# Forty-five products of constants taken out of a fused two-block transformer kernel

## The chip, the cores and the metric

The kernel runs on one NeuronCore of a Trainium2 chip. The metric is device time in microseconds (us) of one launch, the median of several runs. Matrix products run on TensorE (PE in the profile, its weight loads PEld), element-wise work on VectorE (DVE) and ScalarE (ACT); SyncE (SP) issues the transfers of weights.

## What is computed

All in float32, 256 tokens of width 1024. The first block runs four recurrent branches on the same input, merges them by gates, adds the result to the input and normalises it (layer norm 1); a mixture of 32 experts (4 per token) and a gated projection of a side input follow, and layer norm 2. The second block puts 16 learned tokens in front (272 in all) and runs two layers, each half a gated feed-forward network, a mixer (sparse attention and retention in the first, sliding-window attention and pooling in the second, "odd" one), and half a network again. What matters here, from the reference:

```
def _layernorm(x, g, b, dtype):
    xf = x.astype(F32)
    xc = xf - jnp.mean(xf, -1, keepdims=True)
    var = jnp.mean(xc * xc, -1, keepdims=True)
    return (xc * lax.rsqrt(var + LN_EPS) * g + b).astype(dtype)
...
    logits = (xf @ router_w + router_b).astype(F32)
    top_val, top_idx = lax.top_k(logits, TOP_K)
```

## The kernel before

Activations lie transposed in the on-chip memory: 128 partitions of features, 8 tiles deep (`DT`), tokens along the free axis. The program is a list of stages (`STAGES`); each ends in `end_stage` (L771), where PE, ACT and DVE drain and wait for each other. Inside a stage every engine has a list of its own, in the order written, and the lists meet only at semaphores (`Signal`: `post` and `take`).

All large weights are one stream of 2 MB chunks, which SP puts into a ring in the order of use (L3305 for the first stages, L3335 and L3339 for the rest). SP waits before each chunk until PE has left its place; PE waits for a chunk at its first tile (`Weights.take`). So PE pulls the transfers after it, or is held by them. Nearly every product against weights is recorded at L307, in the helper `matmul`. Each product of float32 operands appears in the trace as two MATMUL passes, each with a weight load.

**A layer norm** (`LayerNorm`, L657). PE sums the features by products with a matrix of ones (L673), DVE centres (L700), ACT squares (L687), PE sums the squares, again with ones (`square_sums`, L677, recorded at L681). Then comes a chain off PE: DVE adds the epsilon (L705), ACT takes the root (L689), DVE inverts (L707), DVE scales the eight tiles (L710), and ACT adds beta to each tile (L694).

`idle_products` (L766, recorded at L769) multiplies a constant matrix of ones by a constant identity, 128x128 by 128x128, into a bank of the accumulators in which nothing is kept at that moment. It waits for nothing, posts nothing, and nothing reads what it writes. It is called in three places:

- `merge_and_router` (stage 5, L1828): 13 products after the square sums of layer norm 1. Next on PE is `gate(0)`. It waits for each tile k of the normalised x, multiplies it for both halves of the tokens with the router's weights (stationary x, 32 columns: four passes, L1837), and multiplies the gate's weights with it (256 columns: two passes, L307). Seven more gates follow (`gate(1)` to `gate(7)`) without router products. The experts stage comes next.
- `second_norm` (stage 7, L2307): 28 products after the square sums of layer norm 2. Next on PE is the end of the stage, then the first feed-forward network (`swiglu`), whose products wait for x times a gain (DVE, L2365).
- `odd_mixer` (L3199): 4 products, after one projection step that PE does beside (`beside.next`, L307), and in front of the wait for the normalised queries and keys and of the attention (`attn.tensor`, its first products at L2514).

Of the kernel before, what the change touches and what calls it, by code (L numbers as in the profile page):

```python
# [19 lines left out]
P = 128  # L20
# [271 lines left out]
def new_signal(K, name):  # L292

    sem, count = K.spare.pop() if K.spare else (K.new_semaphore(name), 0)
    K.counts.append(Signal(sem, count))
    return K.counts[-1]
# [8 lines left out]
def matmul(K, out, lhsT, rhs, start, stop, signal=None):  # L305

    ins = K.nc.tensor.matmul(out, lhsT, rhs, start=start, stop=stop)  # L307
    if signal is not None:
        ins.then_inc(*signal.post())
    elif K.weights.pending is not None:  # L310
        ins.then_inc(K.weights.used[K.weights.pending], 1)
        K.weights.pending = None
    return ins
# [176 lines left out]
def flat(ap):  # L490
    return ap.rearrange("p a t -> p (a t)")
# [222 lines left out]
class HeadNorm:  # L714
# [45 lines left out]
    def spread_to(self, dve, j):  # L760

        dve.wait_ge(*self.ready.take())
        return self.K.bank[self.banks[j % len(self.banks)]][:, 0:T2]


def idle_products(K, bank, n):  # L766

    for _ in range(n):
        K.nc.tensor.matmul(K.bank[bank][:, 0:P], K.con["ones"][:, :], K.con["eye"][:, :], start=True, stop=True)  # L769


def end_stage(K):

    K.stages += 1
    n = K.stages
    recycle(K)

    @K.block.tensor
    def _(pe):
        pe.drain().then_inc(K.stage_done, 1)  # L780
        pe.wait_ge(K.stage_done, 3 * n)

    @K.block.scalar
    def _(act):
        act.drain().then_inc(K.stage_done, 1)
        act.wait_ge(K.stage_done, 3 * n)

    @K.block.vector
    def _(dve):
        dve.drain().then_inc(K.stage_done, 1)  # L790
        dve.wait_ge(K.stage_done, 3 * n)

    @K.block.gpsimd
    def _(pool):
        pool.wait_ge(K.stage_done, 3 * n)
# [21 lines left out]
def load(K, pairs):  # L817
    @K.block.gpsimd
    def _(pool):
        for dst, src in pairs:  # L820
            pool.dma_start(dst, src).then_inc(K.small_loaded, 16)
    K.small_loads += len(pairs)
# [948 lines left out]
def merge_and_router(K):  # L1771

    nc, block, bank, col = K.nc, K.block, K.bank, K.col
    T = T1
    with ExitStack() as st:
# [28 lines left out]
        eye = K.con["eye"][:, :]  # L1804
# [5 lines left out]
        def _(pe):  # L1810
# [13 lines left out]
            for j in range(DT):  # L1824
                for k in range(2):
                    matmul(K, p_at(j), K.weights.take(pe), p_in[:, k, :], k == 0, k == 1, p_ready if j == DT - 1 and k == 1 else None)
            ln.square_sums(pe)
            idle_products(K, 6, 13)  # L1828

            def gate(j):  # L1830
                if j >= 2:
# [439 lines left out]
def second_norm(K):  # L2271

    nc, block, bank, col = K.nc, K.block, K.bank, K.col
    with ExitStack() as st:
        ln = LayerNorm(K, st, "l2", K.acc[:, :, :], 4, 5, 1e-5)
        link = new_signal(K, "l2_dve_chain")
        load(K, [(K.x[:, :, 0:META], K.dram["meta"])])
        loads = 16 * K.small_loads
        turned, added = new_signal(K, "l2_turned"), new_signal(K, "l2_added")

        def out(j):
            return K.x[:, j, META:T2]

        @block.tensor
        def _(pe):
            def turn(q):
                for j in (2 * q, 2 * q + 1):
                    for b in range(2):
                        ins = nc.tensor.transpose(bank[q][:, j % 2 * T1 + b * P:j % 2 * T1 + (b + 1) * P], K.moe[:, b, j * P:(j + 1) * P],
                                                  K.con["eye"][:, :])  # L2290
                ins.then_inc(*turned.post())

            def mean(q):
                pe.wait_ge(*added.take())
                ln.mean(pe, 2 * q)
                ln.mean(pe, 2 * q + 1)

            turn(0)
            turn(1)
            mean(0)  # L2300
            turn(2)
            mean(1)
            turn(3)
            mean(2)
            mean(3)
            ln.square_sums(pe)
            idle_products(K, 6, 28)  # L2307

        @block.scalar
        def _(act):  # L2310
            ln.squares(act)
            ln.shift(act, out, "ln2_b")

        @block.vector
        def _(dve):
            for q in range(4):
                dve.wait_ge(*turned.take())
                part = flat(K.acc[:, 2 * q:2 * q + 2, :])
                dve.tensor_tensor(out=part, in0=part, in1=bank[q][:, :], op=ALU.add).then_inc(*added.post())
            dve.wait_ge(*added.posted())  # L2320
            ln.centre(dve)
            ln.scale(dve, out, "ln2_g")
            dve.wait_ge(K.small_loaded, loads)
    end_stage(K)
# [805 lines left out]
def odd_mixer(K):  # L3130
    nc, block, bank, col = K.nc, K.block, K.bank, K.col
    T = T2
    with ExitStack() as st:
# [33 lines left out]
        @block.tensor  # L3167
        def _(pe):
            def mix(j):
                pe.wait_ge(*pool_ready.take())  # L3170
                if j >= 2:
                    pe.wait_ge(*mix_free.take())
                nc.tensor.matmul(bank[j % 2][:, 0:T], dmix[:, j, :], pooled[:, j, :], start=True, stop=True).then_inc(*mix_ready.post())

            for j in range(10):
                columns.tensor(pe, 7 - j % 2, first=K.rms.hn_ready if j in (0, 2) else None, x=y if j < 2 else None)
                if j == 4:
                    pe.wait_ge(K.small_loaded, loads)
                if j > 4:
                    heads.gather(pe, j - 5)  # L3180
                if j > 5:
                    mix(j - 6)
            for k in range(DT):
                w = K.weights.take(pe)
                for b, (t0, tn) in enumerate(Q3):
                    matmul(K, bank[v_banks[b]][0:tn, 0:P], hn[:, k, t0:t0 + tn], w, k == 0, k == DT - 1, v_ready if k == DT - 1 else None)
                if k == 1:
                    heads.gather(pe, 5)
                if k == 4:
                    pe.wait_ge(*mix_free.take(2))  # L3190
                    heads.spread(pe, 0)
                if k > 4:
                    heads.spread(pe, k - 4)
            heads.spread(pe, 4)
            heads.spread(pe, 5)
            columns.until(pe, 10)
            beside.next(pe)
            pe.wait_ge(*v_free.take(3))
            idle_products(K, 5, 4)  # L3199
            pe.wait_ge(*qk_ready.take())  # L3200
            attn.tensor(pe)

# [213 lines left out]
```

## Time and profile before

| | |
|---|---|
| median of 3 runs | 2989.92 us |
| lowest, highest | 2985.75, 2990.21 us |
| the profiled execution | 2988.2 us, of which the span is 2986.4 us and 1.8 us lie around it |
| granted TensorE clock over the span | 0.989 |
| busy share of the span: PE, PEld, DVE, ACT, POOL | 97%, 64%, 27%, 12%, 1% |
| instructions | 35599 |

The span is what the trace covers; starts in the rows are us from its beginning. The granted clock is 1.00 for 2.4 GHz and 0.50 for 1.2 GHz. A busy share of PE says that products were under way, not that they ran at the full clock. A stage's loss counts where PE, or what PE waits for, is the chain that sets the end.

### The profile page before, as it was taken

How to read it: one execution, taken by the hardware profiler on the slowest of the kernel's cores; microseconds unless marked ns; L12 is line 12 of the kernel's file. 1: busy time of each engine (PE TensorE's matmuls, PEld its weight loads, DVE VectorE, ACT ScalarE, POOL GpSimd, SP SyncE). 2: the span in 40 equal slices, each digit the busy share in tenths (PEclk: the TensorE clock that was granted, in tenths of full speed). 3: DMA queues.
4: the chain of work that ended last, by engine and by line, in shares of the span. 5: the costliest groups of instructions: out<-in, count | busy, mean ns of one | idle time of the engine just before them, and what ended most of it. 6: DMA issues, size and time to landing. Idle time of an engine off the chain costs nothing.

```text
span 2986.4 us, 35599 instructions
## 1 busy us (share of the span) xinstructions
PE 2899.7 (97%) x14805; PEld 1911.9 (64%) x14806; DVE 817.3 (27%) x1864; ACT 361.6 (12%) x738; POOL 28.6 (1%) x56
## 2 busy tenths in 40 slices
PE   8999999989999999999999999999999999998999
PEld 7867778833333333333338888776788888876887
DVE  2546441222222222222223111642211111034110
ACT  1122320200000000000002000122000000012000
POOL 0000000000000000000000000000000000000000
PEclk9999999999999999999999999999999999999999
DMA  5122234569999999999994334331333333331430
GB/s 202 59 86 103 92 141 153 197 238 422 428 429 428 428 429 428 429 428 428 428 428 163 141 141 153 113 113 65 113 141 141 141 141 141 141 136 70 157 141 15
DMA packets 49532, 654.92 MB, mean 219 GB/s; under 512 B 5841, under 2 KB 8033, under 8 KB 10225
## 3 DMA queue, kind: packets, MB, share of 16 engines
q1 hardware_dynamic: 45248, 642.90, 53.6%
q0 software_dynamic: 3136, 9.38, 1.0%
q8 instruction: 87, 1.43, 0.2%
q10 hardware_dynamic: 1040, 1.05, 0.1%
q14 instruction: 21, 0.16, 0.0%
HBM read 652.26 MB, written 1.05 MB: 219 GB/s over the span
## 4 chain that ended last, share of the span: by engine, by line
PE 85%; DMA 8%; DVE 5%; ACT 1%; issue 1%; PEldq 0%; SPq 0%; DVEq 0%; PEld 0%; ACTq 0%
PE bank L307 72%; DMA weight_ring<-weight_stream 7%; PE bank L1104 2%; PE bank L2115 1%; PE bank L2084 1%; DVE expert_hidden L2216 1%; DVE expert_hidden L2217 1%; PE bank L2106 1%; PE bank L2348 1%; PE bank L1357 0%; ACT expert_y_slots L2162 0%; DVE mlstm_qk L1482 0%; PE bank L728 0%; DMA first_weight_ring<-weight_stream 0%; PE bank L3013 0%
## 5 line engine op out<-in xcount | busy, mean ns | idle before, releaser
L307 PE MATMUL bank<-ffn_x_gained,weight_ring 128*128 128x272 f32 (+1 forms) x2816 | 638.3, 389 | 3.1 <-DVE ffn_x_gained L2365 3.1
L307 PEld LDWEIGHTS bank<-ffn_x_gained,weight_ring 128*128 128x128 f32 x2816 | 534.7, 190 | 105.2 <-DVE ffn_x_gained L2365 4.6
L307 PE MATMUL bank<-weight_ring,expert_x_slots_t 128*64 128x512 f32 x2048 | 459.6, 600 | 3.5 <-DMA weight_ring<-weight_stream 3.5
L307 PEld LDWEIGHTS bank<-weight_ring,expert_x_slots_t 128*64 128x64 f32 x2048 | 141.3, 138 | 318.9 <-issue 306.0
L307 PE MATMUL bank<-x,first_weight_ring 128*128 128x256 f32 x1376 | 315.6, 385 | 20.4 <-DMA first_weight_ring<-weight_stream 12.7
L307 PE MATMUL bank<-ffn_h,weight_ring 128*128 128x272 f32 (+1 forms) x1408 | 322.0, 389 | 2.1 <-DVE ffn_up L2461 2.1
L307 PEld LDWEIGHTS bank<-ffn_h,weight_ring 128*128 128x128 f32 x1408 | 267.2, 190 | 54.0 <-DVE ffn_up L2461 3.8
L307 PEld LDWEIGHTS bank<-x,first_weight_ring 128*128 128x128 f32 x1376 | 261.6, 193 | 62.3 <-issue 23.4
L307 PE MATMUL bank<-weight_ring,expert_hidden_slots_t 128*64 128x512 f32 x1024 | 225.2, 592 | 0.0
L307 PEld LDWEIGHTS bank<-weight_ring,expert_hidden_slots_t 128*64 128x64 f32 x1024 | 73.4, 137 | 146.4 <-issue 123.7
L307 PE MATMUL bank<-even_hn,weight_ring 128*128 128x272 f32 x624 | 155.1, 404 | 0.0
L2226 DVE TENSOR_TENSOR moe_rows<-moe_rows,bank 128x512 f32<-128x512 f32 x128 | 79.4, 682 | 269.0 <-PE bank L2115 269.0
L307 PEld LDWEIGHTS bank<-even_hn,weight_ring 128*128 128x128 f32 x624 | 118.8, 195 | 28.9 <-issue 5.0
L2461 DVE TENSOR_TENSOR ffn_up<-bank,x_rms 128x272 f32<-128x272 f32 (+1 forms) x88 | 38.5, 438 | 273.7 <-PE bank L307 273.7
L2447 ACT ACTIVATE ffn_silu<-ffn_silu 128x272 f32<-128x272 f32 (+1 forms) x88 | 37.5, 426 | 567.1 <-DVE ffn_silu L2459 567.1
L2459 DVE TENSOR_TENSOR ffn_silu<-bank,x_rms 128x272 f32<-128x272 f32 (+1 forms) x88 | 38.5, 438 | 224.5 <-PE bank L307 224.4
L2470 DVE SCALAR_TENSOR_TENSOR x<-bank,x 128x272 f32<-128x272 f32 (+1 forms) x32 | 14.0, 437 | 313.5 <-PE bank L307 313.5
L307 PE MATMUL bank<-expert_b_gu,expert_select 32*64 32x512 f32 x256 | 70.5, 627 | 8.4 <-issue 8.4
L2216 DVE TENSOR_SCALAR expert_hidden<-bank 128x512 f32<-128x512 f32 x32 | 22.1, 692 | 195.8 <-PE bank L307 195.8
L2084 PE MATMUL bank<-x_rows,expert_pick 128*64 128x512 f32 x256 | 69.0, 618 | 0.0
L2115 PE MATMUL bank<-expert_y_slots,expert_spread 64*128 64x512 f32 x256 | 63.6, 615 | 3.5
L2158 ACT ACTIVATE expert_sigmoid<-expert_gate_part 128x512 f32<-128x512 f32 x32 | 20.2, 630 | 343.5 <-DVE expert_gate_part L2212 343.5
(600 smaller groups left out, 2181.9 us busy)
## 6 DMA issues: line engine op xcount, KB each, us to landing
weight_ring<-weight_stream SPq DMA_DIRECT2D x276, 2048.0 KB, 14.5
first_weight_ring<-weight_stream SPq DMA_DIRECT2D x30, 2048.0 KB, 7.8
x<-x_t SPq DMA_DIRECT2D x1, 1024.0 KB, 5.8
out_t<-x ACTq DMA_DIRECT2D x1, 1024.0 KB, 5.4
c_ret_ret_q<-const_ret_q POOLq DMA_DIRECT2D x1, 544.0 KB, 5.0
c_ret_ret_k<-const_ret_k POOLq DMA_DIRECT2D x1, 544.0 KB, 5.6
c_odd_pool_inv<-const_pool_inv POOLq DMA_DIRECT2D x1, 544.0 KB, 3.8
c_hgrn_hgrn_levels<-const_hgrn_levels POOLq DMA_DIRECT2D x1, 512.0 KB, 3.6
```

The source lines that it names most:

```text
L307: ins = K.nc.tensor.matmul(out, lhsT, rhs, start=start, stop=stop)
L1104: ins = nc.tensor.matmul(out(h), lhsT(h), rhs(h), start=start, stop=stop)
L2084: ins = nc.tensor.matmul(bank[3][rows[g], :], pick[:, b, :], K.x_rows[:, b, g * HW:(g + 1) * HW], start=b == 0, stop=b == 1)
L2106: ins = nc.tensor.transpose(bank[5][:, j * P:(j + 1) * P], h[:, 0, j * P:(j + 1) * P], eye)
L2115: ins = nc.tensor.matmul(bank[4 + 2 * b + g][:, :], spread_t[rows[g], b * P:(b + 1) * P], ys[rows[g], :], start=True, stop=True)
L2216: then(dve.tensor_scalar(h[:, 0, :], bank[1][:, :], 7.0, -7.0, ALU.min, ALU.max))
L2217: dve.scalar_tensor_tensor(out=h[:, 0, :], in0=h[:, 0, :], scalar=1.0, in1=gate[:, 0, :], op0=ALU.add, op1=ALU.mult)\
L2226: ins = dve.tensor_tensor(out=part, in0=part, in1=bank[4 + n][:, :], op=ALU.add)
L2348: self.K.nc.tensor.matmul(self.K.bank[6][:, 0:T2], self.K.con["ones"][:, :], self.sq[:, j % 2, :], start=j == 0, stop=j == DT - 1)\
L2447: act.activation(s[:, j % 2, :], s[:, j % 2, :], ACT.Silu).then_inc(*s_ready.post())
L2459: dve.tensor_tensor(out=s[:, j % 2, :], in0=bank[2 * (j % 2)][:, 0:T], in1=rms.rstd[:, t0:T2], op=ALU.mult).then_inc(*g_scaled.post())
L2461: dve.tensor_tensor(out=up[:, j % 2, :], in0=bank[2 * (j % 2) + 1][:, 0:T], in1=rms.rstd[:, t0:T2], op=ALU.mult).then_inc(*h_free.post())
```

## The change

The function and its three calls are deleted. 13, 28 and 4 products go, together 90 MATMUL passes with as many weight loads. Nothing is put in their place; no semaphore, buffer or order of other work is touched.

```
-def idle_products(K, bank, n):
-
-    for _ in range(n):
-        K.nc.tensor.matmul(K.bank[bank][:, 0:P], K.con["ones"][:, :], K.con["eye"][:, :], start=True, stop=True)
...
             ln.square_sums(pe)
-            idle_products(K, 6, 13)
...
             ln.square_sums(pe)
-            idle_products(K, 6, 28)
...
             pe.wait_ge(*v_free.take(3))
-            idle_products(K, 5, 4)
             pe.wait_ge(*qk_ready.take())
```

## Rows read from the trace of the kernel before

**Rows 1.** The page: span, PE, chain that ended last by engine

```profile
span 2986.4 us, 35599 instructions
PE 2899.7 (97%) x14805; PEld 1911.9 (64%) x14806; DVE 817.3 (27%) x1864; ACT 361.6 (12%) x738; POOL 28.6 (1%) x56
...
PE 85%; DMA 8%; DVE 5%; ACT 1%; issue 1%; PEldq 0%; SPq 0%; DVEq 0%; PEld 0%; ACTq 0%
```

**Rows 2.** The source line L769: the deleted products' passes, in ns

```profile
L769 PE MATMUL bank<-c_eye,c_ones x90: 273/275/275, 572.9 to 2690.0; 128*128 128x128 f32 x90
```

**Rows 3.** The chain around layer norm 1: start us, us, what

```profile
569.61 3.47 PE bank L681 x16
...
576.32 0.52 ACT x L694
...
576.88 0.63 PE bank L1837 x4
...
583.66 7.42 PE bank L307 x34
```

**Rows 4.** Windows there: length, busy by engine, then PEclk, DMA share, GB/s

```profile
575.95:576.87 0.92, 0.01 (x1) 0.00 (x0) 0.92 (x3) 0.56 (x2) 0.00 (x0) 1.00 0.01 0
576.88:583.66 6.78, 6.78 (x47) 6.42 (x48) 2.17 (x6) 4.02 (x8) 0.00 (x0) 1.00 0.67 242
```

**Rows 5.** Windows of the experts stage

```profile
660.00:663.00 3.00, 3.00 (x10) 0.77 (x8) 0.00 (x0) 0.00 (x0) 0.00 (x0) 0.50 0.00 0
...
700.00:1577.00 877.00, 861.21 (x3924) 283.33 (x3921) 230.07 (x545) 75.69 (x126) 0.95 (x1) 1.00 1.01 428
```

**Rows 6.** The chain around layer norm 2

```profile
1571.77 3.73 PE bank L681 x16
...
1582.72 4.39 PE bank L307 x18
```

**Rows 7.** The chain from there, its longest piece

```profile
1593.99 106.10 PE bank L307 x463
```

**Rows 8.** Windows of the second norm's deleted products

```profile
1575.10:1581.75 6.65, 6.64 (x58) 6.41 (x56) 5.43 (x10) 3.43 (x9) 0.00 (x0) 1.00 0.29 121
```

**Rows 9.** The chain in front of the odd attention

```profile
2686.81 0.51 DVE odd_cq_ck L3239
2687.36 1.99 PE bank L307 x8
2689.36 0.89 PE bank L769 x8
2690.25 0.47 PE bank L2514 x4
```

**Rows 10.** Windows where PE sits idle and the clock then falls

```profile
653.40:658.10 4.70, 0.00 (x0) 0.00 (x0) 3.02 (x10) 0.00 (x0) 0.00 (x0) 1.00 0.94 397
658.20:665.00 6.80, 6.02 (x14) 1.56 (x16) 0.48 (x2) 0.00 (x0) 0.00 (x0) 0.50 0.22 51
```

**Rows 11.** Windows on both sides of other falls and rises

```profile
310.00:310.80 0.80, 0.80 (x6) 0.80 (x6) 0.00 (x0) 0.00 (x0) 0.00 (x0) 0.50 0.00 0
310.85:316.70 5.85, 5.85 (x15) 4.68 (x16) 0.00 (x0) 0.18 (x1) 0.00 (x0) 0.50 0.00 0
...
1558.00:1562.60 4.60, 1.79 (x8) 0.49 (x6) 2.56 (x7) 0.33 (x1) 0.00 (x0) 1.00 1.01 431
1562.70:1566.00 3.30, 2.99 (x11) 2.48 (x12) 1.38 (x2) 0.00 (x0) 0.95 (x1) 0.50 0.99 422
...
1857.60:1863.00 5.40, 5.40 (x15) 4.13 (x13) 0.97 (x4) 0.00 (x0) 0.00 (x0) 0.50 0.01 3
...
2699.35:2706.10 6.75, 5.51 (x21) 3.76 (x18) 5.04 (x19) 2.89 (x12) 0.00 (x0) 0.50 0.00 0
...
2729.50:2733.40 3.90, 3.90 (x9) 3.18 (x10) 0.07 (x1) 0.00 (x0) 0.00 (x0) 0.50 0.00 0
```

**Rows 12.** Groups by line and form, 306.5 to 309.9 us: an 8-column product

```profile
L1541 PE MATMUL bank<-mlstm_w_gates,x 128*128 128x8 f32 x28 | 3.3, 257 | 1.3 <-PEq L780 1.3
```

## The prediction

> **What bounds the kernel now.** I read the page first. PE is busy for 97% of the span and holds 85% of the chain that ended last; DMA holds 8%, all other engines 7% [rows 1]. So the question at each of the three places is whether PE is on the chain there, and at what clock it runs. The line of the deleted products shows 90 passes of 275 ns [rows 2]. They overlap: eight of them take 0.89 us of the chain [rows 9], 0.111 us each, so the three groups last about 2.9, 6.2 and 0.9 us.
>
> Then I read the chain at each place. At the first norm PE ends the square sums at 573.08 (569.61 + 3.47) and reappears on the chain at 576.88 with the router's products, released by ACT's first tile at 576.84 [rows 3]. The 3.80 us between belong to DVE and ACT; the 13 products lie beside that chain, and PE is idle for only 0.92 us after them, with the clock at 1.00 [rows 4]. At the second norm PE ends the sums at 1575.50 and reappears at 1582.72, 7.2 us later; DVE's and ACT's steps and at last the stage's end are the chain between [rows 6], and the 28 products run beside them at full clock and end before 1581.75 [rows 8]. In front of the odd attention it is otherwise: DVE ends the last query tile at 2687.32, PE the projection step at 2689.35, and the four products stand on the chain for 0.89 us until the attention's first product at 2690.25 [rows 9].
>
> Last, the granted clock. After each of the first two places PE alone is the chain for long: `gate(0)` fills 6.78 us, all busy and at 1.00 [rows 4], the next gates follow at once [rows 3], and behind the second norm one piece of PE's chain runs for 106.1 us [rows 7]. A low clock there is paid in full.
>
> **The change, part by part.** What goes from the chain directly is 0.89 us at the odd attention [rows 9]. What is late next there is nothing on another engine: the queries were ready 2 us earlier, PE goes straight from the projection step to the attention. At the norms the direct gain is nothing: DVE and ACT cover the products, and they do the same work without them. What the products do is keep PE streaming, so I price the clock.
>
> *Does it fall?* Twice the trace shows PE going idle and the clock then falling: PE's last product in one case ended near 1559.8 and the clock was 0.50 from about 1562.7, 2.9 us later [rows 11]; in the other it ended near 653.4 and the clock was still 1.00 until 658.1, 4.7 us later, and 0.50 from then on [rows 10]. The second norm's 7.2 us exceed both: it falls there before PE resumes. The first norm's 3.80 us lie between the two: it falls within the wait or up to 0.9 us after `gate(0)` begins. I take 0.5 us.
>
> *What does low clock cost?* At 0.50, 15 passes of the gates' kind (128x256) touch 5.85 us [rows 11], about 0.39 us each; at 1.00, 34 took 7.42 us, 0.218 us each [rows 3]. Half of a low stretch is loss.
>
> *How long, where dense products follow?* Where PE resumes with full products, and no narrow ones ran before, the clock rose 3.30 and 3.90 us into them; where they followed a run of narrow products, of 8 columns in the case at 310 us, only 5.40 and 5.85 us into them [rows 11]. Half of that is 1.6 to 2.9 us. For the second norm I take 2.2 us, inside the two ends, nearer to the dense ones that it resembles.
>
> *How long in `gate(0)`?* It isn't dense: of its six passes per tile four have 32 columns. The nearest rows stand on two sides. The dense resumptions above give half of 3.3 us, 1.6 us. On the other side, 28 passes of 8 columns, each with a weight load of 128, kept PE busy for 3.3 us before 309.9 us [rows 12], and the clock fell while they ran, to 0.50 at 310.0, and stayed there through the remaining ones and 5.85 us of dense work [rows 11]. Being busy alone didn't help there. Were the clock held low for all of `gate(0)`, its 6.78 us [rows 4] would double: +6.8 us, less 0.5 us for the late fall, and then the dense gates would run low for a while, 1.6 to 2.9 us more, of which I take 2.3. That is 8.6 us, with 7.4 and 9.7 as ends. A pass of 32 columns with a 128-column weight load is nearer to the 8-column ones than to the dense ones in how little it streams between loads, so I take this side.
>
> The Trainium skill, "TensorE: Matmul & The Clock Gate", section "What's actually happening", has the gate follow how busy PE has recently been, and says beside it that instructions aren't counted; read so, the unbroken stream of `gate(0)` would release the clock as dense work does, and the first norm would cost 1.6 instead of 8.6 us. The 8-column stretch differs from that reading, since the clock fell under it. The sum below stands without this paragraph.
>
> *Is the first norm's loss absorbed?* From 700 to 1577 us the transfers run at 428 GB/s without a break [rows 5]: the experts are bound by DMA. But at 660 to 663 us nothing is transferred while PE works [rows 5]; the ring is full and SP waits for PE. The continuous stretch begins when PE frees places, so a late PE makes it begin late, and end late. No absorption: the loss before it is carried whole. From 1577 us on the ring is full again, and PE sets the pace.
>
> *Clock in the odd attention.* It already falls twice there, with 6.75 us low the first time, 5.51 of them busy [rows 11]. In front of the wait the four products make way for the attention's first scores and the next dense step, so PE streams about as much. I take no change; a fall that comes earlier and lasts once more would cost half of 5.51, 2.8 us, so this place gives -0.9 to +1.9 us.
>
> **Sum:** 8.6 + 2.2 - 0.9 = +9.9 us. Against the profiled execution's own 2988.2 us that is 2998.1 us; the median of the runs lies 1.7 us higher, which gives 2999.8. I forecast 2999 us. A measurement of this kernel can tell about 0.2%, 6 us, from no change.
>
> **Rivals.** *The clock comes back within `gate(0)`.* Its products leave no gap, and the wide ones are half of its time. Against it stand the 8-column stretch and the long rise after it. It gives 1.6 + 2.2 - 0.9 = +2.9 us, 2991 us (ends +2.3 and +4.9 with each norm at 1.6 to 2.9). This is also the time by the skill's rule named above. It decides if in the changed trace the clock is 1.00 before the last router product.
>
> *Not slower: the clock doesn't fall at the first norm, and what falls at the second is small.* The wait of 3.80 us is shorter than the 4.7 us for which an idle PE kept its clock [rows 10], and at the second norm the first products wait for DVE tile by tile, which could cover part of a slow start. Then only the third place counts: -0.9 us, 2987.3 us. It needs the fall to come later than 3.80 us at the first norm and `gate(0)` to hold the clock once reached, and at the second norm a loss under 0.9 us. That is against the 7.2 us, so the second norm's 1.6 us are likely even here, and the case would end near +0.7.
>
> *The change does something else.* The products post no signal and nothing reads their banks, so no order changes. I give it nothing of its own.
>
> **How the numbers follow.** The clock held low through `gate(0)`: 0.58, at +9.9 us, own range +8.1 to +11.8 (7.4 + 1.6 - 0.9 to 9.7 + 2.9 - 0.9), up to +14.6 if the odd attention adds its 2.8. It comes back early: 0.30, at +2.9. Nothing or almost nothing lost: 0.12, at -0.9 to +0.7. The range of 8 in 10 goes from 2989, which takes in most of the second case and leaves out the third, to 3003 (2988.2 + 14.6). The likeliest case's own range is 2996 to 3002. Slower by over 0.2% is the first case, 0.57. Within 0.2% are the other two, 0.41. No case reaches -6 us; 0.02 is left for it.
>
> **What would show it.** The windows of the changed trace should show PEclk 0.50 from 576.9 us, or within 1 us of it, to past the last router product, `gate(0)` lasting 12 to 13.6 instead of 6.8 us, and the rise some us into `gate(1)`; a start of the experts about 8 us later, and the steady 428 GB/s shifted by as much; again 0.50 from PE's return after the second norm for 3.3 to 5.9 us; and at the odd attention a chain with the projection step followed at once by L2514. The forecast is wrong if the clock is at 1.00 before the router's products end, if the experts start less than 4 us later, or if the end of the experts hasn't moved with their start.

## The result: slower by 8 us, the clock low for 17 us at the first norm

The changed kernel takes 2997.87 us (median of 19 launches, 2993.45 to 3006.01) against 2987.47 us for the kernel before in the same 19 rounds (2984.53 to 3001.02). The ratio of the two kernels over all launches is 1.0027, with a 95% interval of 1.0018 to 1.0037, that is +8.1 us, +5.4 to +11.1; the medians lie 10.4 us apart. The forecast was 2999 us.

The profiled execution took 2994.5 us. Of its page:

```profile
span 2992.7 us, 35420 instructions
PE 2897.1 (97%) x14715; PEld 1908.1 (64%) x14716; DVE 816.9 (27%) x1864; ACT 362.1 (12%) x738; POOL 28.6 (1%) x56
```

90 passes are gone, which took 10.0 us together, but PE is busy for only 2.6 us less than in [rows 1], and the span is 6.3 us longer. The busy shares say nothing of where it went. The windows do (length, busy time of PE, PEld, DVE, ACT and POOL, then PEclk, DMA share, GB/s):

```profile
575.50:576.90 1.40, 0.29 (x3) 0.29 (x3) 1.38 (x4) 0.86 (x3) 0.00 (x0) 1.00 0.06 23
577.00:593.90 16.90, 16.90 (x56) 14.74 (x56) 4.56 (x20) 4.03 (x8) 0.00 (x0) 0.50 0.34 125
594.10:620.00 25.90, 25.90 (x133) 20.99 (x131) 8.91 (x28) 7.59 (x14) 0.00 (x0) 1.00 0.22 82
1585.10:1587.20 2.10, 0.00 (x0) 0.00 (x0) 1.61 (x2) 0.42 (x1) 0.00 (x0) 1.00 0.02 8
1587.40:1592.30 4.90, 0.00 (x0) 0.00 (x0) 4.03 (x11) 3.72 (x10) 0.00 (x0) 0.50 0.00 0
1592.30:1597.40 5.10, 5.10 (x11) 3.87 (x12) 1.85 (x7) 0.34 (x2) 0.00 (x0) 0.50 0.48 154
```

In the second line PE is busy the whole time, at half its clock. Read by itself the busy column would call that stretch perfect. The chain shows what it cost (start us, us, what):

```profile
569.34 3.47 PE bank L681 x16
...
576.61 0.79 PE bank L1830 x4
577.39 1.01 PE bank L307 x2
578.41 0.69 PE bank L1830 x4
...
589.34 9.79 PE bank L307 x34
...
629.78 18.65 PE bank L307 x72
...
1592.30 6.96 PE bank L307 x18
```

`gate(0)`, from the first router product to the long piece behind it, takes 12.73 us (576.61 to 589.34) against the 6.78 us of [rows 3]: +5.95. A tile costs 1.70 us, 1.01 for the two wide passes and 0.69 for the four narrow ones. The next 34 dense passes take 9.79 us against 7.42: +2.37. The experts begin at 629.78, 8.0 us after the 621.8 of the kernel before, of which the place itself made 8.3 (the launch was 0.3 us ahead at the norm). Behind the second norm 18 passes take 6.96 us against the 4.39 of [rows 6]: +2.57.

In front of the odd attention the chain of the changed kernel runs from the projection step into the attention's first product with nothing between, as forecast:

```profile
2697.22 3.78 PE bank L307 x8
2701.00 0.81 PE bank L2506 x4
```

But here the step itself ran at low clock, 3.78 us against the 1.99 of [rows 9]. The windows of this stage:

```profile
2696.70:2703.40 6.70, 6.18 (x16) 4.44 (x17) 1.86 (x7) 0.00 (x0) 0.00 (x0) 0.50 0.00 0
2703.50:2740.00 36.50, 30.07 (x209) 20.43 (x208) 24.00 (x91) 14.51 (x56) 0.00 (x0) 1.00 0.16 59
```

In the kernel before the clock was low twice here, from 2699.35 and again to 2733.40 [rows 11]; now once, and earlier, over the projection step itself. The attention and what follows it come out shorter.

Where the 6.9 us are by which the store of the output starts later, from the first starts of the tiles' instructions in each stage, for the attention's end from the last start (kernel after minus kernel before, us): -0.3 before the first norm, +8.3 at it, +0.2 in the experts, +1.4 in front of the second norm's wait, +2.6 behind it, 0.0 in the first network, -2.7 in the even mixer, +0.3 to the odd mixer, +0.9 in its first part, -1.5 in its attention, -2.3 behind that.

### The profile page after: what moved, and what is told of

Read it like the earlier page. It is cut to its first block, busy times and chain, and to the rows that moved or that the text cites. A ratio compares the mean times of both kernels' runs of the same rounds, so it can differ in the third digit from the quotient of the medians.

```text
span 2992.7 us, 35420 instructions
## 1 busy us (share of the span) xinstructions
PE 2897.1 (97%) x14715; PEld 1908.1 (64%) x14716; DVE 816.9 (27%) x1864; ACT 362.1 (12%) x738; POOL 28.6 (1%) x56
## 4 chain that ended last, share of the span: by engine, by line
PE 86%; DMA 8%; DVE 4%; ACT 1%; issue 1%; PEldq 0%; SPq 0%; DVEq 0%; PEld 0%; ACTq 0%
PE bank L307 73%; DMA weight_ring<-weight_stream 7%; PE bank L1098 2%; PE bank L2108 1%; PE bank L2077 1%; DVE expert_hidden L2209 1%; DVE expert_hidden L2210 1%; PE bank L2099 1%; PE bank L2340 1%; PE bank L1351 0%; ACT expert_y_slots L2155 0%; PE bank L728 0%; DMA first_weight_ring<-weight_stream 0%; PE bank L738 0%; PE bank L3005 0%
## 5 line engine op out<-in xcount | busy, mean ns | idle before, releaser
L307 PE MATMUL bank<-x,first_weight_ring 128*128 128x256 f32 x1376 | 322.3, 391 | 20.4 <-DMA first_weight_ring<-weight_stream 12.8
L307 PEld LDWEIGHTS bank<-even_hn,weight_ring 128*128 128x128 f32 x624 | 115.8, 190 | 27.5 <-issue 5.0
```

## Experiments

The parts are named by what they add at a place in the trace (the difference of the shifts at its two ends) and by the ratio of the launches, since launches scatter: the standard deviation of a set is 2.0 to 6.1 us. Line numbers differ by up to 9 between kernels; the operands tell which product it is.

**The first norm's 13 products alone, twice.**

```
             ln.square_sums(pe)
-            idle_products(K, 6, 13)
```

> Only the 13 products after the first norm's square sums are taken out; the other 32 stay. Theory (the clock falls in the 3.8 us wait and stays low through all of gate(0) and some us beyond): +8 us against the kernel before, gate(0) 12 to 13.6 us long, the experts 8 us later, the second norm and the odd attention as before. Rival (a mere restart of the clock after the wait): +1.6 us, gate(0) 8.5 us.

> Again only the 13 products at the first norm taken out, in a second set of launches and a second trace. The first trace lost 7.8 us at the place, the first set of launches only 1.8 us (interval -2 to +6). Theory (the loss at the place is 6 to 8.5 us in nearly every alignment, and the other low stretches scatter around it): the trace again shows about 17 us low and the experts 6 to 8 us later against the end of the square sums; launches +4 to +9 us. Rival (in many alignments the clock doesn't fall there, and the traces were bad luck): a trace without it, or launches again under +3 us.

Both traces show it. Windows of the first set's trace, in the wait and behind it, then of the second's:

```profile
576.60:579.40 2.80, 0.00 (x0) 0.00 (x0) 2.25 (x3) 0.42 (x1) 0.00 (x0) 1.00 1.01 433
579.50:596.50 17.00, 16.09 (x54) 14.21 (x55) 5.44 (x22) 4.97 (x10) 0.00 (x0) 0.50 0.34 124
```

The second:

```profile
573.50:576.55 3.05, 0.00 (x0) 0.00 (x0) 2.53 (x3) 0.42 (x1) 0.00 (x0) 1.00 0.94 403
576.70:593.60 16.90, 16.32 (x54) 14.40 (x55) 5.31 (x22) 4.97 (x10) 0.00 (x0) 0.50 0.36 125
```

17 us low each time, +7.8 and +8.0 us from the norm to the experts. The theory's place and price hold. The launches say less: ratios 1.0006 (0.9993 to 1.0019) and 1.0022 (1.0012 to 1.0031), +1.8 and +6.6 us. The +8 us expected of the first set lie outside its interval; the second set is inside the +4 to +9 expected of it. In both traces some of it comes back: between the first network's sums of squares and the store of the output the first kernel's shift goes from 12.2 to 6.0 us, the second's from 9.2 to 3.1, because low stretches of the kernel before in the odd attention are missing. In neither was the attention's clock ever low.

**The second norm's 28 alone.**

```
             ln.square_sums(pe)
-            idle_products(K, 6, 28)
```

> Only the 28 products after the second norm's square sums are taken out. Theory (the clock is low for 3.3 to 5.9 us of dense work after the 7.2 us wait, and half of that is loss): +1.6 to +2.9 us, with the first 18 passes behind the norm at 6 to 7 instead of 4.4 us. Rival (the first products wait for VectorE anyway, which covers the low clock): under +0.9 us.

Ratio 1.0016 (1.0000 to 1.0032), +4.8 us, with an interval that begins at no change. The chain:

```profile
1585.62 6.97 PE bank L307 x18
```

That is +2.58 against [rows 6], inside 1.6 to 2.9. VectorE's tile by tile release covers none of it. The rival falls. Later in this trace the odd attention has more low clock than in the kernel before, 20.7 against 13.8 us, and the way from the odd mixer's start to the attention's first product is 2.6 us longer.

**The odd attention's 4 alone.**

```
             pe.wait_ge(*v_free.take(3))
-            idle_products(K, 5, 4)
```

> Only the 4 products in front of the odd attention are taken out. Theory (they stand on the chain and keep nothing up): -0.9 us, the attention's first product straight after the projection step. Rival (they keep the clock up in the attention): the low stretches in it start earlier or last longer, up to +1.9 us. The time of a launch scatters by more than either, so the trace decides.

Ratio 0.9999 (0.9986 to 1.0011). In the trace:

```profile
2689.99 1.99 PE bank L307 x8
2691.98 0.47 PE bank L2514 x4
```

The 0.89 us of [rows 9] are gone: the shift falls from +2.6 us at the odd mixer's start to +1.7 at the attention's. By the attention's end it is back at +2.1, with the clock low twice for 6.8 us as before. The local gain is shown; a gain of the launch isn't.

**Thirteen narrow products in place of the wide ones.**

```
+def narrow_products(K, bank, n):
+
+    for _ in range(n):
+        K.nc.tensor.matmul(K.bank[bank][:, 0:8], K.con["ones"][:, :], K.con["eye"][:, 0:8], start=True, stop=True)
...
             ln.square_sums(pe)
-            idle_products(K, 6, 13)
+            narrow_products(K, 6, 13)
```

> The 13 products after the first norm's square sums keep their place, number, weights and time (0.11 us a pass), but have 8 columns instead of 128, so PE is as busy and streams a sixteenth. Nothing else is changed. Theory (what keeps the clock is what PE streams, not that it is busy): as without them, the clock falls around gate(0)'s start and +8 us. Rival (the Trainium skill, TensorE: Matmul & The Clock Gate, What's actually happening, read as busy time): the clock stays at 1.00 and the time is that of the kernel before.

Ratio 1.0021 (1.0009 to 1.0033), +6.3 us. The source line of the narrow products:

```profile
L775 PE MATMUL bank<-c_eye,c_ones x26: 173/256/256, 578.4 to 581.1; 128*128 128x8 f32 x26
```

The windows over them and behind them:

```profile
578.40:581.35 2.95, 2.95 (x27) 2.86 (x25) 2.25 (x3) 0.42 (x1) 0.00 (x0) 1.00 1.00 428
581.50:598.40 16.90, 16.04 (x54) 14.15 (x55) 5.34 (x22) 4.97 (x10) 0.00 (x0) 0.50 0.35 126
```

PE is busy for all of 2.95 us and loads weights for 2.86 of them. With the wide products of the kernel before it was the same:

```profile
572.95:575.95 3.00, 3.00 (x27) 2.82 (x25) 2.33 (x3) 0.42 (x1) 0.00 (x0) 1.00 1.01 431
```

Yet the clock falls, before the wait is over: +7.7 us to the experts, as without any product. In all eight traces with the 13 wide products in place, of the kernel before and of variants that leave them alone, the clock is 1.00 from 566 to 600 us; in this one and in the three with none of them in front of an unchanged `gate(0)` it is 0.50 for 17 us. The forecast had left this to a choice. The number, the loads and the time are nearly equal; what differs is the columns that a pass streams, 8 in place of 128. It is one trace, and the launches agree with it.

**The router's products moved out of the way**, in the changed kernel:

```
                     if j == 0:
                         pe.wait_ge(*ln.ready.take())
+                    if j == 1:
                         for b in range(2):
```

> The changed kernel, with the 32 router passes of 32 columns moved from gate(0) to gate(1); gate(0) is then dense. No product of constants anywhere. Theory (the router's narrow passes hold the clock low once it has fallen; dense work brings it back in 3.3 to 3.9 us): the clock rises inside gate(0) or at the latest early in gate(1), the low stretch at the first norm is 3.4 to 7 us long instead of 17.1, the experts start 2 to 3.5 us later than in the kernel before instead of 8.0, and the launch takes about 5 us less than with the change alone. Rival (the length of the low stretch comes from the 3.8 us wait or from chance): again 17 us low and +8 us.

The windows around its low stretch:

```profile
579.00:585.70 6.70, 5.72 (x14) 4.55 (x15) 3.16 (x8) 4.58 (x9) 0.00 (x0) 0.50 0.55 181
585.80:600.00 14.20, 14.20 (x87) 12.99 (x86) 5.28 (x24) 5.23 (x9) 0.00 (x0) 1.00 0.14 60
```

The clock falls in the same wait and comes back after 5.8 us of dense work (PE resumes at 579.98), later than the 3.3 to 3.9 us expected, but inside `gate(0)`; the router's passes then run at full clock in `gate(1)`. +2.8 us to the experts in place of 8.3. Launches: 1.0008 (0.9998 to 1.0018), against 1.0027 with the change alone; 5.7 us less by these ratios, about 5 were expected. So the fall belongs to the wait, and that it lasts 17 us and not 7 belongs to the narrow products behind it.

**Half of the products.**

```
-            idle_products(K, 6, 13)
+            idle_products(K, 6, 6)
...
-            idle_products(K, 6, 28)
+            idle_products(K, 6, 14)
```

> The kernel before with 6 instead of 13 products at the first norm and 14 instead of 28 at the second, so PE idles for about 2.4 us and 4.1 us in front of the next work instead of 0.9 and 1.0; the 4 in front of the odd attention stay. Theory (the clock falls after 2.9 to 4.7 us of idle PE): it stays up at the first norm in this execution or most, it may fall at the second; time within 2 us of the kernel before. Rival (any idle part of that size in front of narrow products is enough): the clock falls at the first norm and the experts start up to 8 us later.

The trace is as the theory has it, the launches aren't. In the trace `gate(0)` runs at full clock, and the second norm loses 1.7 us:

```profile
577.00:583.50 6.50, 6.50 (x46) 6.14 (x46) 2.15 (x6) 4.00 (x8) 0.00 (x0) 1.00 0.70 239
...
1583.10:1586.40 3.30, 3.30 (x9) 2.41 (x8) 1.30 (x5) 0.00 (x0) 0.00 (x0) 0.50 0.60 149
```

But the 12 launches have a ratio of 1.0029 (1.0016 to 1.0042), +8.7 us, as much as with all products gone; the profiled one, 2993.2 us, is among the three fastest. "Time within 2 us" is refuted. That 2.4 us of idle PE are enough in most launches, the rival, fits the number; no trace of such a launch was caught, so it is not shown. Another cause stands beside it: this trace itself lost time elsewhere. Of its 5.7 us at the store 2.7 arise between the odd mixer's start and the attention's first product, where PE's clock was low from 2688.9:

```profile
2689.65 3.78 PE bank L307 x8
2693.43 1.71 PE bank L769 x8
```

The projection step and the four products of constants took 1.99 and 0.89 us in [rows 9]. Which of the two the launches pay for stays open.

**Three attempts at something faster than both.** Products after the last expert's, where PE waits for VectorE, and none at the odd attention:

```
             K.weights.at += EXPERT_TILES * (NE - 1)
+            idle_products(K, 1, 11)
...
-            idle_products(K, 5, 4)
```

> The kernel before without the 4 products in front of the odd attention, and with 11 products after the last expert's, where PE waits 3.2 us for VectorE and the clock fell at 1562.7 us. Theory: the clock is 1.00 through the second norm's turning and sums of means, which saves half of the 3.4 or 6.8 us of low clock seen there in five traces, 1.7 to 3 us, and the 0.9 us at the attention: -2.6 to -4 us in the mean. Rival (the products only delay the stage's end, or the clock falls there in any case): 0 to -0.9 us.

Ratio 1.0001 (0.9990 to 1.0013). In its trace no low stretch begins between 664 and 1861 us, and the second norm comes 1.0 us sooner after the experts, the attention 0.9 us sooner. The launches show neither, and the expected -2.6 to -4 us lie outside the interval.

The router's passes for the second half of the tokens in `gate(1)`, in the kernel before:

```
-                        for b in range(2):
-                            ins = nc.tensor.matmul(bank[4 + b][:, 0:NE], x[:, k, b * P:(b + 1) * P], rw[:, k, :], start=k == 0, stop=k == DT - 1)
-                        if k == DT - 1:
+                    if j < 2:
+                        ins = nc.tensor.matmul(bank[4 + j][:, 0:NE], x[:, k, j * P:(j + 1) * P], rw[:, k, :], start=k == 0, stop=k == DT - 1)
+                        if j and k == DT - 1:
```

> The kernel before, all 45 products in place, with the router's passes for the first 128 tokens in gate(0) and those for the other 128 in gate(1), so each tile has two narrow passes and two wide ones. Question: where do the launches of the kernel before at 2998 to 3001 us come from (10 of 54, against a median near 2989)? Theory: in some alignments the clock falls at the first norm in spite of the products, because of the narrow passes behind the short idle time, and stays low until gate(1); then these launches go away here and the mean falls by 1 to 3 us, the lowest times staying as they are. Rival (they come from the attentions' low stretches): the same share of launches some 10 us above the lowest.

Ratio 0.9994 (0.9984 to 1.0003), highest launch 2995.0. The kernel before, in its 34 launches beside it (a 35th, of 9888 us, is left out; its cause is unknown), had only one at 2997.6 or above, so the missing slow launches prove nothing. Inconclusive. And all three edits together:

> The kernel before with the router's passes spread over gate(0) and gate(1), without the 4 products in front of the odd attention, and with 11 products after the last expert's; the 41 at the norms stay. If the parts add as their traces say (1 to 2 us in the mean, 0.9 us, 1 us): -2.5 to -4 us against the kernel before, ratio 0.9987 to 0.9992. Rival (the parts measured apart are all noise): a ratio of 1.000.

Ratio 1.0007 (0.9998 to 1.0016), not faster; the expected 0.9987 to 0.9992 are refuted. None of the three expected gains is shown by the launches; no version was found that is shown to beat the kernel before.

**The kernel before, unchanged.**

> The kernel before, unchanged, for another trace and as a measure of what two sets of launches of one program differ by. Question: does its clock sometimes fall at the first norm in spite of the 13 products? Theory (the alignment of the work to the chip's own watching of PE differs from launch to launch): the low stretches around 227, 310, 1562, 1856, 2050, 2100, 2700 and 2730 us differ in length and presence by 3.4 us or multiples; a ratio within 0.15% of 1. Rival (a launch's low stretches are fixed by the program): the same ten stretches as in the first trace.

> The kernel before, unchanged, for a third trace; as the run before it. If this trace or that one has a low stretch that begins between 573 and 584 us plus what the launch is late by then, the launches at 2998 to 3001 us are explained.

Ratio 1.0001 (0.9992 to 1.0011) for the first; the second took 2989.8 us in its one launch. Neither clock is low at the first norm. The two share with the first trace the low stretches near 310, 621, 658, 1856, 1952, 2048, 2099, 2700 and 2727 us; what differs is the length of that at 310 (6.8 us, or 3.4 and a second of 3.4 at 331) and that at 1562, which is in the first trace only. The launches at 2998 to 3001 us are not explained; at 2998 us or above there were 4 in 19 launches, then 4 in 35 (6 with the two at 2997.9 and 2998.0), then none in 34 and in 27.

## Why the prediction was right, point by point

*What bounds the kernel.* Right. At both norms the products lay beside the chain, and taking them away freed nothing there: in both stages what waited for DVE and ACT started no sooner.

*It falls.* Right. At the first norm PE's last product ended at 572.8 and the clock was 0.50 from 576.95, 0.3 us into `gate(0)`, where 0.5 us had been taken. In the three other traces without wide products before an unchanged `gate(0)` it fell 0.7 to 1 us before `gate(0)`, inside the wait. At the second norm it fell between 1587.2 and 1587.4, 2.2 us after the last product and 4.9 us before PE returned; the rows of before had given 2.9 us as the shortest delay, so that bound was too high, without an effect on the sum.

*The low clock lasts through `gate(0)`.* Right, and this was the step with the chance of 0.58. Forecast 6.8 - 0.5 us for it, measured 5.95; forecast 2.3 us for the dense gates behind, measured 2.37 (low for about 4.7 us of them). The sum of 8.6 came out at 8.3, and at 7.7 to 8.0 in three other traces. The reason given, that narrow products don't keep the clock, was a choice between two rows; the narrow products in place of the wide ones and the router's products moved away each agree with it.

*The rival in which the clock comes back within `gate(0)`* fell: +2.9 us in all was its price, and 8.3 came from that place alone. The clock did come back within `gate(0)` once the narrow products were out of it, at +2.8 us for this place; the rival had priced the place at 1.6 us, with 2.9 as its upper end. The Trainium skill, "TensorE: Matmul & The Clock Gate", section "What's actually happening", speaks of how busy PE has been; the 26 narrow passes at full busy time differ from that, if busy is read as the busy column of a profile.

*No absorption by the experts' transfers.* Right: 8.0 us late at their start, 8.2 at their end, and the rate again 428 GB/s between (the kernel after's window, against [rows 5]):

```profile
700.00:1577.00 877.00, 862.48 (x3915) 280.00 (x3912) 228.77 (x548) 72.16 (x120) 0.95 (x1) 1.00 1.01 428
```

*The second norm.* Mis-sized within its bounds: 2.2 us taken, 2.57 and 2.58 measured. The rise came about 5.2 us into the dense work, not 3.3 to 3.9; the choice of "nearer to the dense ones" was the poorer one. With the 5.8 us of the moved router products that is twice that dense work needed longer than the two dense rows had it, so 3.3 and 3.9 us were no bound.

*The odd attention.* The -0.9 us is there where it is measured alone, and there "I take no change" for the clock held too. In the kernel after it didn't: the first part lost 0.9 us, since the projection step ran at the low clock, which cost more than the four missing products saved, and one low stretch less gave back 1.5 and 2.3 us behind it. The upper bound of +1.9 us looked only in one direction; a gain should have stood beside it.

*The sum.* +9.9 us against +8.1 in the launches and +6.3 in the traced spans. Some of its ends are off by 0.1 us (9.7 + 2.9 - 0.9 is 11.7, not 11.8, so the upper end is 14.5), which changes nothing. The two norms' 10.9 us came true at their places, where 10.8 were forecast. Two terms were put at nothing: the low stretch in front of the second norm, at 1562 us before and at 1570 after, grew from 3.5 to 6.9 us (+1.4 us), and what came back later was 5.3 us in the kernel after between the first network and the store, 6.2 and 6.1 in the first norm's two traces, but nothing in the narrow-products kernel (11.9 us late there, 12.0 at the store). That it comes from the low stretches of the mixers is shown by the windows: between 1842 and 2750 us the clock is low for 38.0 us in the kernel before and for 27.5 in the kernel after, and half of the difference is 5.3. Whether an upstream delay makes those stretches fewer in the mean, or these traces were alike by chance, stays open; a delay isn't needed, since with the router's passes spread, 0.2 us late at the odd attention, both stretches there are missing too. That 2999 us came within 1.1 us of the median is in part luck: it started from a median of 3 launches, 2989.9 us, where 19 gave 2987.5. In the launches the two parts of the norms, +1.8 and +6.6 for the first and +4.8 for the second, add up to the whole within their intervals.

## What to carry to other kernels

Where PE waits several us for other engines and long PE work follows, filler products are worth what the low clock would cost behind the wait, not what they take: here 3 us of products beside the chain saved 7.7 to 8.3 us at their place, and 1.8 and 6.6 us in two sets of launches. Look at what comes first after the wait: here a mix with narrow products stayed at the low clock until it ended and 4.7 us longer, and with the dense work first the place lost 2.8 us in place of 8.3. Make the filler wide, and don't shorten it on the word of one trace. Read PEclk beside the busy share, and trust a place's own difference for its price and many launches for the total; single traced launches of these kernels lay from 5.5 us under to 5.1 us over the median of their own set.

## What the hardware showed that was not expected

- 26 passes of 8 columns that kept PE busy for 2.95 of 2.95 us left the clock to fall as an idle PE did; 26 passes of 128 columns over the same 3 us kept it, in eight traces of eight.
- A mix of two passes of 256 and four of 32 columns kept a clock of 1.00 for 6.78 us in the kernel before and, entered after the fall, did not bring it back in 12.3 us. The same work ran at either level here, at the one at which it was entered.
- Six products in place of 13 and 14 in place of 28 showed full clock at the first norm in one trace and, in 12 launches, cost as much as none at all; why is open.
